# Selected attention in a two-block transformer kernel: where a unit's first two items are turned and copied

## The reference

```python
k_blocks = rmsnorm(k_s, k_norm_g)...            # 8 blocks of 64 tokens; 16 may be selected, so all are
sc = jnp.einsum('bcgrd,bgcnld->bgrcnl', q_b, k_sel) + bias
p = masked_softmax(sc, mask, axis=(-2, -1))
o_slc = jnp.einsum('bgrcnl,bgcnld->bcgrd', p, v_sel)
...
o = gt[..., 0:1] * o_cmp + gt[..., 1:2] * o_slc + gt[..., 2:3] * o_win
```

## Time and profile before

| | |
|---|---|
| median of 3 runs | 1952.48 us (1948.31 to 1954.78) |
| the profiled execution | 1951.42 us |
| its span | 1949.6 us |
| mean granted TensorE clock | 0.98 |
| TensorE busy | 1844.8 us, 95% of the span |
| VectorE, ScalarE, GpSimd busy | 774.8, 436.1, 1270.8 us |
| the attention's eight units | about 1150 to 1298 us |

### The profile page before, as it was taken

One profiled execution on the slowest core, in us unless ns is written; L12 is line 12 of the kernel. 1 busy time (PEld: TensorE's weight loads), 2 busy tenths in 40 slices (PEclk: granted clock), 3 DMA queues, 4 the chain that ended last, 5 costly groups with the idle time before them and its releaser, 6 DMA issues.

```text
span 1949.6 us, 29753 instructions
## 1 busy us (share of the span) xinstructions
PE 1844.8 (95%) x11700; PEld 1467.9 (75%) x11700; DVE 774.8 (40%) x1348; ACT 436.1 (22%) x885; POOL 1270.8 (65%) x621
## 2 busy tenths in 40 slices
PE   6999999988779999999899999998879999999998
PEld 4888888856557888888577786676776878888887
DVE  4333351164655333311313434415755435555301
ACT  3000011034522000000212245634444121212000
POOL 6888888844075888888566643242365867777773
PEclk8999999989899999999999999999999999999999
DMA  4222233221021222233332351131005323222331
GB/s 154 95 94 96 102 94 95 81 91 65 12 87 56 95 96 97 93 99 100 132 130 85 121 181 58 55 140 45 4 17 219 97 77 96 97 97 94 98 93 61
DMA packets 58779, 180.32 MB, mean 92 GB/s; under 512 B 6931, under 2 KB 13843, under 8 KB 58172
## 3 DMA queue, kind: packets, MB, share of 16 engines
q1 hardware_dynamic: 49132, 165.83, 25.4%
q10 hardware_dynamic: 9552, 13.13, 1.9%
HBM read 165.81 MB, written 13.13 MB: 92 GB/s over the span
## 4 chain that ended last, share of the span: by engine, by line
PE 89%; DVE 6%; ACT 3%; issue 2%; DMA 0%; ACTq 0%; SPq 0%; DVEq 0%
PE bank L546 25%; PE bank L548 25%; PE bank L547 25%; PE bank L596 2%; PE bank L911 1%; PE bank L864 1%; PE bank L897 1%; DVE h_lo L1698 1%; PE bank L828 1%; PE bank L1069 1%; ACT p2T L1510 0%; DVE tmp L1742 0%; DVE xT L1745 0%; DMA prm<-params_dram 0%; PE bank L647 0%
## 5 line engine op out<-in xcount | busy, mean ns | idle before, releaser
L454 POOL TENSOR_TENSOR w_hi<-w_raw,one 128x1024 fp32r<-128x1024 f32 (+1 forms) x279 | 525.7, 1884 | 546.2 <-PE bank L548 535.5
L456 POOL TENSOR_TENSOR w_lo<-w_raw,w_hi 128x1024 fp32r<-128x1024 f32 (+1 forms) x279 | 691.9, 2480 | 21.9
L546 PE MATMUL bank<-h_hi,w_hi 128*128 128x512 f32 x1528 | 620.5, 406 | 27.4 <-DVE h_lo L1698 12.4
L547 PE MATMUL bank<-h_lo,w_hi 128*128 128x512 f32 x1528 | 598.5, 392 | 0.0
L548 PE MATMUL bank<-h_hi,w_lo 128*128 128x512 f32 x1528 | 598.1, 391 | 0.0
L546 PEld LDWEIGHTS bank<-h_hi,w_hi 128*128 128x128 f32 x1528 | 288.7, 189 | 110.6 <-issue 29.5
L547 PEld LDWEIGHTS bank<-h_lo,w_hi 128*128 128x128 f32 x1528 | 289.1, 189 | 67.8 <-issue 10.1
L548 PEld LDWEIGHTS bank<-h_hi,w_lo 128*128 128x128 f32 x1528 | 288.8, 189 | 61.1
L546 PE MATMUL bank<-a_hi,w_hi 128*128 128x512 f32 x528 | 205.6, 389 | 0.0
L548 PE MATMUL bank<-a_hi,w_lo 128*128 128x512 f32 x528 | 205.6, 389 | 0.0
L547 PE MATMUL bank<-a_lo,w_hi 128*128 128x512 f32 x528 | 205.6, 389 | 0.0
(11 more groups left out here) (347 smaller groups left out, 1953.6 us busy)
## 6 DMA issues: line engine op xcount, KB each, us to landing
w_raw<-w_ffn_gu_dram SPq DMA_DIRECT2D x88, 512.0 KB, 3.4
w_raw<-w_conv_up_dram SPq DMA_DIRECT2D x44, 512.0 KB, 3.5
w_raw<-w_ffn_down_dram SPq DMA_DIRECT2D x32, 448.0 KB, 3.2
w_raw<-w_ffn_down_dram SPq DMA_DIRECT2D x16, 512.0 KB, 3.5
w_raw<-w_out_dram SPq DMA_DIRECT2D x16, 512.0 KB, 3.4
w_raw<-w_gates_dram SPq DMA_DIRECT2D x16, 512.0 KB, 3.6
w_raw<-w_rwkv_dram SPq DMA_DIRECT2D x14, 512.0 KB, 3.5
w_raw<-w_conv_down_dram SPq DMA_DIRECT2D x16, 448.0 KB, 3.3
```

What stands on the lines that cost most here:

```text
L454: nc.gpsimd.tensor_tensor(w_hi[:, s, 0:width], raw, one[:, 0:1].to_broadcast([P, width]), ALU.mult).then_inc(sem("w_rounded"), 1)
L456: nc.gpsimd.tensor_tensor(w_lo[:, s, 0:width], raw, w_hi[:, s, 0:width].bitcast(F32), ALU.subtract).then_inc(sem("w_split"), 1)
L546: nc.tensor.matmul(dst, hi, rhs_hi[:, k, :], start=start and k == k0, stop=False)
L547: nc.tensor.matmul(dst, hi, rhs_lo[:, k, :], start=False, stop=False)
```

## The change

A unit's first two items are no longer turned in `nsa_weigh`, behind the fill. `turn_first` turns them within the next unit's score run, between scores 5 and 6; for the last unit, which has no next one, ahead of its fill. ScalarE copies them (`copy_items(n, 0, 2)`) behind the next unit's exponentials and ahead of `fill_out`. The other items keep their places. The number of instructions of each kind is the same.

```diff
--- before.py
+++ after.py
@@ -852,10 +852,12 @@
             pe.wait_ge(*nth("nsa_read", 17))
             pe.wait_ge(*nth("kc_normed", 1))
 
-            def nsa_scores(n, g, unit):
+            def nsa_scores(n, g, unit, ahead=None):
 
 
                 for i in range(10):
+                    if i == 6 and ahead:
+                        ahead()
                     b = bank[i % 4] if unit % 2 == 0 else bank[(i + 2) % 4]
                     if 10 * unit + i >= 4:
                         pe.wait_ge(*nth("nsa_masked", 10 * unit + i - 3))
@@ -876,6 +878,27 @@
 
             turn = [0]
 
+            def nsa_items(n):
+                return [(v, j) for v in range(2) for j in range(n + 1)] + [(2, 0)]
+
+            def turn_item(n, g, unit, x):
+
+                v, j = nsa_items(n)[x]
+                k = turn[0] + x
+                if k >= 2:
+                    pe.wait_ge(*nth("p2T_ready", k - 1))
+                for h in range(4):
+                    src = Ec[:, unit % 2, h, 0:8 * n + 7] if v == 2 else E[:, unit % 2, 4 * v + h, j * P:(j + 1) * P]
+                    rows = 8 * n + 7 if v == 2 else P
+                    last = nc.tensor.transpose(bank[4 + k % 2][0:rows, h * P:(h + 1) * P], src, flip)
+                last.then_inc(sem("nsa_turned"), 1)
+
+            def turn_first(n, g, unit):
+
+                pe.wait_ge(*nth("nsa_weighed", unit + 1))
+                for x in range(2):
+                    turn_item(n, g, unit, x)
+
             def nsa_weigh(n, g, unit):
 
 
@@ -883,19 +906,7 @@
                 dst = bank[6][:, c0:c0 + 2 * P]
                 if unit >= 2:
                     pe.wait_ge(*nth("nsa_out_read", unit - 1))
-                items = [(v, j) for v in range(2) for j in range(n + 1)] + [(2, 0)]
-                pe.wait_ge(*nth("nsa_weighed", unit + 1))
-
-                def turn_item(x):
-                    v, j = items[x]
-                    k = turn[0] + x
-                    if k >= 2:
-                        pe.wait_ge(*nth("p2T_ready", k - 1))
-                    for h in range(4):
-                        src = Ec[:, unit % 2, h, 0:8 * n + 7] if v == 2 else E[:, unit % 2, 4 * v + h, j * P:(j + 1) * P]
-                        rows = 8 * n + 7 if v == 2 else P
-                        last = nc.tensor.transpose(bank[4 + k % 2][0:rows, h * P:(h + 1) * P], src, flip)
-                    last.then_inc(sem("nsa_turned"), 1)
+                items = nsa_items(n)
 
                 def sum_item(x):
                     v, j = items[x]
@@ -913,10 +924,9 @@
                     last.then_inc(sem("p2T_used"), 1)
                     return last
 
-                turn_item(0)
                 for x in range(len(items)):
-                    if x + 1 < len(items):
-                        turn_item(x + 1)
+                    if 2 <= x + 1 < len(items):
+                        turn_item(n, g, unit, x + 1)
                     last = sum_item(x)
                 turn[0] += len(items)
 
@@ -925,7 +935,9 @@
             fill()
             for u, (n, g) in enumerate(units):
                 if u + 1 < len(units):
-                    nsa_scores(*units[u + 1], u + 1)
+                    nsa_scores(*units[u + 1], u + 1, lambda: turn_first(n, g, u))
+                else:
+                    turn_first(n, g, u)
                 fill()
                 nsa_weigh(n, g, u)
 
@@ -1498,17 +1510,20 @@
 
             turn = [0]
 
-            def nsa_copies(n, g, unit):
-                items = 2 * (n + 1) + 1
-                c0 = 2 * P * (unit % 2)
-                for x in range(items):
+            def copy_items(n, first, end):
+                for x in range(first, end):
                     k = turn[0] + x
                     act.wait_ge(*nth("nsa_turned", k + 1))
                     if k >= 2:
                         act.wait_ge(*nth("p2T_used", k - 1))
-                    rows = 8 * n + 7 if x == items - 1 else P
+                    rows = 8 * n + 7 if x == 2 * (n + 1) else P
                     nc.scalar.activation(p2T[0:rows, k % 2, :, :].rearrange("p h t -> p (h t)"),
                                          bank[4 + k % 2][0:rows, :], ACT.Copy).then_inc(sem("p2T_ready"), 1)
+
+            def nsa_copies(n, g, unit):
+                items = 2 * (n + 1) + 1
+                c0 = 2 * P * (unit % 2)
+                copy_items(n, 2, items)
                 turn[0] += items
                 act.wait_ge(*nth("p2T_used", turn[0]))
                 nc.scalar.activation(oA[:, 2 * g:2 * g + 2, n * P:(n + 1) * P],
@@ -1524,6 +1539,7 @@
             for u, (n, g) in enumerate(units):
                 if u + 1 < len(units):
                     nsa_exps(*units[u + 1], u + 1)
+                copy_items(n, 0, 2)
                 fill_out()
                 nsa_copies(n, g, u)
 
```

## The result

The changed kernel takes 1940.8 us in the median of 5 runs (1938.58 to 1942.0), against 1952.48 us before (5 runs, 1948.31 to 1954.78). The ratio is 0.9945, with a 95% interval of 0.9935 to 0.9955: 0.55% faster; the medians differ by 11.7 us. The forecast was 1941.5 us, faster.

A forecast was written before the change was run, and what follows sets the result against it. TensorE, busy 95% of the span, was taken as the bound. Removing 17.0 us, less 4.5 for score runs and 1.1 for the last unit, gave 11.4, rounded to 11: 1941.5 us, 8-in-10 range 1937.5 to 1947.5.

The forecast's parts named there:

- Removed: 17.0 us: Behind the fill, two turned items and the wait before the first sum go, 2.13 us in each of eight units.
- Added to the score runs: 4.5 us, between 2.3 and 6.7: Seven score runs gain eight transposes each, partly hidden in TensorE's waits for VectorE's masks; the middle value was taken.
- upper bound: Score runs: score 5 alone holds the array for double time, with 0.17 us gaps around the turns; 6.7 us added at most.
- rival B: Score runs: transposes hide nothing, each unit saves 0.94 us, together 7.5 us, giving 1945.0 us; chance 0.14.
- The rule on weight loads: Score runs: by the skill, loads overlap matmuls only in different row groups, so the transposes' load would wait for score 5.
- The last unit: 1.1 us: No next score run, so its turns stand ahead of its fill, costing 1.02 us, or 1.19 with a gap.
- lower bound: Whole stage: smallest gain 7.7 us, with a gap at each sum and the dearest score runs and last unit.
- A: Whole kernel: the forecast itself, 1941.5 us, within 1938.8 to 1944.8; chance 0.68.
- Cover on ScalarE: Between last exponential and fill's end, at least 2.4 us (n = 3) to hold two copies of 1.2 us.
- The waits that were to cost nothing: The wait for the weights, now with scores 6 to 9 and a fill queued behind it, and for earlier copies: no cost.
- Rival C: After the stage or before the first sum, the gain is given back through a DMA or late copies: about 1952 us; chance 0.12.
- Rival D: Fills: longer short work ahead drops the clock to 1.2 GHz, 5.4 us per fill; four give 1963 us; chance 0.06.

The follow-up runs named there:

- all three places tried: Turns between scores 5 and 6 (the changed kernel, 1940.8 us), or moved from there to between 3 and 4 (1941.49 us) or 7 and 8 (1942.57 us, one run).
- the other two: Two repetitions of the unedited changed kernel against the kernel before: 1942.6 us against 1950.03 (ratio 0.9962) and 1943.24 us against 1952.08 (0.9950).
- late_copies: Changed kernel with ScalarE's copies of items 0 and 1 put back behind the fill's copy and DMA issue, turns still early: 1960.83 us, ratio 1.0044 to before.

## Why the prediction was right, point by point

- *The bound.* Right. The wait was on TensorE's path: with 8.4 us out of the stage the span shrank by 9.5. Of these, 1.6 us lie ahead of the stage, where nothing was changed, and behind it the span is 0.7 us longer; both are within what the ten traces scatter.
- *Removed: 17.0 us.* Mis-sized; measured 14.4. I let the first sum follow the fill like the first turn did, with 1.4 us as the bound's allowance for a gap. The gap is there in all eight units: from the fill's first load to what follows it is 5.67 us with a sum behind it and 5.35 with a turn, so 8 x 0.33 = 2.6 us.
- *Added to the score runs: 4.5 us, between 2.3 and 6.7.* Measured 5.1, nearer to the upper bound. At n = 3 its terms, where 4.43 us in all stood against a measured 4.22: score 5 and its gap 1.06 (0.86 + 0.17), turns to the next score 1.02 (1.02 + 0.17), scores 6 to 9 1.53 (0.86 + 0.75); the 0.61 from score 4 to score 5 is as forecast. The waits for masks were filled as both bounds had it. What separates the bounds is the price of a lone score and of the gaps beside the turns; the middle value took half of it, and about two thirds of it came. On balance a pair costs 0.82 us in the open and 0.60 to 0.89 in the run, so rival B, "the transposes hide nothing", was nearly right; its price of 1.19 us a pair was too high.
- *The rule on weight loads.* By the Trainium skill, "TensorE: Matmul & The Clock Gate", Part 3, the transposes' load should wait for a score that uses some of its rows. Here the trace agrees: 0.76 us of idle load time, in all three places tried behind a score of 512 columns. For the fill it does not the earlier trace rows; the same section names a load into a background weight buffer as a second case that may overlap, and no run here tells which loads are such. The upper bound, which lets the turns wait for score 5, was the better one.
- *The last unit: 1.1 us.* Measured 0.8.
- *Sum: 11.4 us.* The stage gave 8.4: 2.6 less for the gap behind the fill, 0.6 less for the score runs, 0.3 more for the last unit. That is nearer to rival B's 7.5 than to the forecast, and above the 7.7 of the lower bound. The predicted time of 1941.5 us against 1940.8 was so close by luck, since the first comparison held about 3 us that did not repeat; against the other two, 1942.6 and 1943.24, it is low by 1 to 2 us. Whole runs can't tell A from B here; the stage can.
- *Cover on ScalarE.* Right: mask 6 came late (VectorE waited 0.85 us at n = 3), the exponentials took it up but for 0.26 us, and 1.71 us were left between the two copies and the fill's copy.
- *The waits that were to cost nothing.* Right; the third item's copy is not waited for, and the sums take as long as before.
- *Rival C.* Not seen: the part behind the stage is as long as before within the scatter, and its longest wait for a transfer, of VectorE for the reloaded inputs, stood there before (31.4 us) and is 28.7 us now. *Rival D.* Not in this kernel: the windows over all its units show 1.00. The Trainium skill, "TensorE: Matmul & The Clock Gate", Part 4, says that transposes don't count as busy for the clock in the same way. These rows don't bear it out for transposes mixed with other work: in the last unit a fill is followed by 9.5 us of transposes and small sums in turn, at 1.00. For transposes alone no run here shows it. The only falls in the stage, in any of the ten traces, were the two in late_copies, each behind an idle stretch.

## What to carry to other kernels

When a step is moved into another engine's waiting time, look at what stands just ahead of it: a step that needs the whole array first waits for a lone half-array matmul to end (0.76 us here), and a wait filled early can come back later in the same paced run. When a consumer waits, undo the producer's move and the copy's move one at a time: here neither early turns (1.0044) nor early copies (0.9968) gave the gain of both. And measure an effect of half a percent in its stage, from start to start in the trace, before believing the third digit of a ratio.

## What the runs showed of the hardware that was not expected

Eight transposes (two items) take 1.02 us of loads behind a fill, 0.85 us elsewhere, and add 0.82 us to the path when they stand ahead of a fill. In late_copies the clock fell to its lower level 1.3 and 1.4 us after TensorE had resumed from idle stretches of 1.84 and 1.83 us (at the first, 0.54 and 0.61 in the two windows behind it), not during them, and each fall cost 1.5 us; of eight such idle stretches in that trace (1.69 to 1.84 us) two were followed by it. Outside the stage, identical work took 1809.5 to 1814.6 us.
